# Hybrid decoder step on one core: sample tokens' projections on two column halves, their attention placed between halves of the output projection, first stage reordered

## The chip, the cores and the metric

The kernel runs on one NeuronCore of a Trainium2 chip. The core has TensorE (PE: matrix products and transposes), VectorE (DVE), ScalarE (ACT), GpSimd (POOL) and SyncE (SP, here only an issuer of transfers), each with its own instruction stream. They share SBUF (128 partitions), eight PSUM banks of 128 x 512 f32 and 16 DMA engines, and wait for each other through semaphores. All data is f32, so a product of 512 columns leaves two records of about 0.43 us. The metric is device time in microseconds of one execution; lower is better.

## The reference, cut to what is computed

One layer for two groups of tokens: a prompt of 512 tokens (one sequence) and 64 sample tokens (8 sequences of 8 tokens with stored states). Width 1024, 4 retention heads of 128.

```
mod = silu(c) @ w_mod + b_mod                       # per sequence: sh1 sc1 g1 sh2 sc2 g2
u = rmsnorm(x, n_pre1) * (1 + sc1) + sh1
z = u @ w_in;  xr, yg, q, k, v, g = split(z)
out_a = rglru(causal_conv(xr)) * gelu(yg)           # 512 channels
q, k = rotary(q) * DK**-0.5, rotary(k)
o, s_last = retention(q, k, v, s0)                  # per head, see below
out_b = groupnorm(o) * ret_gn_w * silu(g)
x = x + g1 * rmsnorm(concat(out_a, out_b) @ w_out, n_post1)
u2 = rmsnorm(x, n_pre2) * (1 + sc2) + sh2
x = x + g2 * rmsnorm(moe(u2), n_post2)              # top-2 of 4 in one of 4 groups, 16 experts
```

Retention in chunks of c tokens (128 in the prompt, 8 in a sample sequence), with decay gamma of the head:

```
inner = (q k^T * mask) v
cross = q s0 * gamma^(i+1)                          # s0: 128 x 128 state of the sequence and head
s_last = gamma^c * s0 + k^T (w_state * v)
```

For the sample tokens there are 8 sequences x 4 heads = 32 states (2 MB) to read, use and write.

## The kernel before

**Tiling.** Tokens lie in TILES = 5 tiles: four of 128 prompt tokens, and tile 4 with NS = 64 sample tokens. `x` holds them by rows, `uT` transposed, 128 channels by 576 tokens, in 8 channel steps (KT). Weights stream through `ring`, nine slots of 1 MB; SyncE issues the loads in the fixed order of `weight_pieces`, each as soon as the piece that held its slot is used up.

**The stages on TensorE** (each engine's instructions are written out in its own order; there is no scheduler):

1. First stage. Transposes of the set-up rows into bank 0, `turn_x` for each tile, `scale_part(h, i)` and `scale_sum(h)` (scale and shift of the first norm, two halves h of the channels, four parts each, with 32-row operands `cT` on four column groups of the array), `first_tiles(h)` (24 products of 288 tokens by 128 channels: channel tiles 0 to 2 of the convolution input, channel half h). Then in turn `gate_products(m)` (64x64 blocks of the RG-LRU gates), `by_channel(c, m)` (16 products of 288), `mod_step(gq, k)` (the other modulation rows, in two groups gq of 8 steps, accumulated in bank 4). VectorE runs `conv`, `rg_lru`, `gated` and `mod_rows` in a fixed order; `mod_rows(1)` empties bank 4 and frees it for `mod_step(2, 0)`.
2. Projections. For tile t and c = 0 to 3 (q, k, v, g), `project(t, c)`: 8 products with the tile's tokens stationary and 512 weight columns moving. Between them the attention of tile t-1: `turn_qk`, `scores`, `outputs`, `turn_out`. ScalarE's `take` empties the banks, VectorE's `rotate`, `mask`, `advance` and `group_norm` follow.
3. Attention of tile 4, once `turn_out(3)` is issued: `turn_qk(4)`, `scores(4)`, `sample_outputs`. The last goes head by head: one product with v, 8 of 8 columns with the states `s0` (two buffers, so GpSimd loads state h only when h-2 is stored), 2 of 512 columns for the state's increment from `vblk` (v of the 64 tokens spread over 8 blocks). VectorE's `sample_states` adds and scales, then TensorE transposes the result back, `group_norm(4)`, `turn_out(4)`.
4. Output. `out_proj(t)`: two halves c of 8 products of 512 (row names `hy`, `outbT`), then `turn_u2(t-1)`: 8 transposes, a wait for ScalarE's `take_u2T`, and 8 router products of 20 columns (row names `wrt,uT`). ScalarE's `square_m`, `square_x` and VectorE's `after_mixer(t)` make `x` and `u2` of the tile; `after_mixer(0)` also waits for all state stores (`s_ssto`).
5. Routing, then 16 experts of 128 slots each, gather of the two results per token, and the last norm.

Lines L632 and L635 are the helpers `mm` and `turn` that issue every product and transpose; L1068 is the helper of every ScalarE operation.

## Time and profile before

| | us |
|---|---|
| median of 3 runs | 695.72 (691.23 to 701.94) |
| the profiled execution | 693.1 |
| its span, first to last instruction | 691.3 |
| TensorE busy | 586.9 (85%) |
| VectorE busy | 216.2 (31%) |
| ScalarE busy | 168.6 (24%) |
| GpSimd busy | 85.2 (12%) |
| DMA, over the span | 131.45 MB, 190 GB/s |

The page divides the span into 40 slices of 17.3 us, and names the chain of work that ended last. A row of the timeline gives start, duration, engine, line, operation, output<-inputs (program's names), form and count; in brackets the idle time of the engine just before it and what ended it. `arena` is the shared work space in which most temporary tiles lie.

### The profile page before, as it was taken

The page shows a single profiled execution, that of the slowest core. Times are in us where ns is not written, and L with a number is a line of the kernel's source. Part 1 is how long each engine was busy: PE and PEld are TensorE (multiplying, and loading weights), DVE is VectorE, ACT ScalarE, POOL GpSimd, SP SyncE. Part 2 cuts the span into 40 slices and gives each one's busy share as a digit, 9 for nine tenths or more (in the row PEclk, how much of TensorE's full clock was granted, in tenths as well). Part 3 has the DMA queues.
Part 4 walks back from the last instruction along what each step waited for, and adds up shares of the span by engine and source line. Part 5 has one row for each costly group of instructions (what it writes and reads, how often), then busy time and mean ns, then how long its engine had stood idle before and what let it go on. Part 6 is the DMA issues. An engine that isn't in the chain of part 4 may idle for free.

```text
span 691.3 us, 6321 instructions
## 1 busy us (share of the span) xinstructions
PE 586.9 (85%) x2385; PEld 358.8 (52%) x2385; DVE 216.2 (31%) x495; ACT 168.6 (24%) x326; POOL 85.2 (12%) x123
## 2 busy tenths in 40 slices
PE   1897997999999999987798889339999999999700
PEld 1565654544545453465344443228777777777400
DVE  2514664120333241423314222541212121312137
ACT  3602875012222222210112211311111111112143
POOL 3104000072000000033000000220101010100060
PEclk9899999999999999955599999659999999999955
DMA  9999366794000003853200000825999999993283
GB/s 313 368 337 287 123 243 244 261 350 147 1 0 1 0 1 121 282 173 107 62 0 40 22 30 30 305 63 186 348 344 379 356 361 357 370 358 135 91 271 138
DMA packets 65155, 131.45 MB, mean 190 GB/s; under 512 B 4287, under 2 KB 37239, under 8 KB 63075
## 3 DMA queue, kind: packets, MB, share of 16 engines
q1 hardware_dynamic: 53264, 94.64, 39.0%
q0 software_dynamic: 8080, 23.15, 10.9%
q10 hardware_dynamic: 3778, 13.23, 4.9%
q8 instruction: 21, 0.34, 0.2%
q14 instruction: 12, 0.09, 0.0%
HBM read 115.32 MB, written 15.69 MB: 190 GB/s over the span
## 4 chain that ended last, share of the span: by engine, by line
PE 80%; DVE 7%; ACT 4%; DMA 4%; issue 2%; POOL 1%; DVEq 0%; POOLq 0%; ACTq 0%
PE bank L632 76%; PE bank L635 5%; ACT arena L1068 3%; DMA hy<-in_norm_pre_mix_dram 1%; DMA arena<-slots_dram,tok_slot 1%; ACT uT L1068 1%; DVE arena L1758 1%; DMA arena<-in_state_ret_dram 1%; DMA arena<-u_dram,slot_tok 1%; DMA out_dram<-arena 1%; DVE arena L1880 1%; ACT ss L1068 0%; DVE rtb L1701 0%; ACT L1068 0%; POOL arena L620 0%
## 5 line engine op out<-in xcount | busy, mean ns | idle before, releaser
L632 PE MATMUL bank<-ring,arena 128*128 128x256 f32 (+1 forms) x640 | 173.3, 427 | 2.1 <-DVE arena L1839 1.3
L1068 ACT ACTIVATE arena<-bank 128x512 f32<-128x512 f32 (+5 forms) x117 | 54.1, 493 | 364.1 <-PE bank L632 340.4
L632 PEld LDWEIGHTS bank<-ring,arena 128*128 128x128 f32 x640 | 120.3, 192 | 38.6 <-issue 25.8
L632 PE MATMUL bank<-ring,uT 128*128 128x512 f32 (+1 forms) x320 | 140.2, 593 | 0.0
L632 PEld LDWEIGHTS bank<-ring,uT 128*128 128x128 f32 (+1 forms) x320 | 56.1, 180 | 72.6 <-issue 72.3
L632 PE MATMUL bank<-uT,ring 128*128 128x288 f32 x256 | 68.6, 431 | 3.1 <-ACT uT L1068 3.1
L632 PEld LDWEIGHTS bank<-uT,ring 128*128 128x128 f32 x256 | 51.1, 202 | 18.8 <-issue 4.1
L635 PE MATMUL bank<-con,arena 128*128 128x128 f32 (+1 forms) x304 | 44.6, 287 | 14.6 <-DVE arena L1673 4.2
L635 PEld LDWEIGHTS bank<-con,arena 128*128 128x128 f32 (+1 forms) x304 | 37.4, 150 | 36.0 <-issue 22.1
L632 PE MATMUL bank<-arena 128*128 128x128 f32 (+4 forms) x216 | 46.7, 367 | 5.1 <-DMA arena<-in_state_ret_dram 3.9
L632 PEld LDWEIGHTS bank<-arena 128*128 128x128 f32 (+2 forms) x216 | 35.9, 246 | 18.6 <-issue 9.0
L632 PE MATMUL bank<-ring,hy 128*128 128x512 f32 (+1 forms) x80 | 44.1, 704 | 0.5 <-issue 0.5
L1068 ACT ACT_TABLE_LOAD x32 | 41.1, 1283 | 6.0 <-issue 5.5
L1864 DVE TENSOR_TENSOR arena<-arena,bank 128x256 f32<-128x256 f32 x16 | 6.7, 422 | 103.4 <-ACT arena L1068 103.4
L632 PE MATMUL bank<-ring,outbT 128*128 128x512 f32 (+1 forms) x80 | 36.0, 592 | 0.0
L609 POOL DMA_INDIRECT arena<-u_dram,slot_tok x16 | 16.4, 1023 | 152.1 <-DVE slot_tok L1833 147.1
L632 PEld LDWEIGHTS bank<-ring,hy 128*128 128x128 f32 (+1 forms) x80 | 16.6, 213 | 23.9 <-issue 23.9
L632 PE MATMUL bank<-ring,rowsT 128*32 128x512 f32 x192 | 23.9, 633 | 3.7 <-DVE arena L1461 3.7
L1068 ACT ACTIVATE arena<-bank,con 128x128 f32<-128x128 f32 (+1 forms) x40 | 11.4, 366 | 59.9 <-PE bank L632 53.0
L1846 DVE COPY arena<-bank 128x512 f32<-128x512 f32 x16 | 11.1, 692 | 46.7 <-PE bank L632 46.7
L632 PEld LDWEIGHTS bank<-ring,outbT 128*128 128x128 f32 (+1 forms) x80 | 14.4, 180 | 20.0 <-issue 20.0
L1652 DVE RECIPROCAL ss<-ss 128x1 f32<-128x1 f32 (+1 forms) x5 | 0.8, 161 | 65.9 <-ACT ss L1068 65.9
(182 smaller groups left out, 405.7 us busy)
## 6 DMA issues: line engine op xcount, KB each, us to landing
ring<-in_w_mod_dram SPq DMA_DIRECT2D x24, 1024.0 KB, 9.6
ring<-in_w_exp_gate_dram SPq DMA_DIRECT2D x16, 1024.0 KB, 13.0
ring<-in_w_exp_up_dram SPq DMA_DIRECT2D x16, 1024.0 KB, 11.7
ring<-in_w_exp_down_dram SPq DMA_DIRECT2D x16, 1024.0 KB, 7.8
ring<-in_w_in_dram SPq DMA_DIRECT2D x12, 1024.0 KB, 14.5
slots_dram<-arena ACTq DMA_DIRECT2D x16, 512.0 KB, 6.9
ring<-in_w_out_dram SPq DMA_DIRECT2D x4, 1024.0 KB, 6.1
x<-in_x_prompt_dram ACTq DMA_DIRECT2D x4, 512.0 KB, 10.2
```

The lines of the kernel that those rows point to most:

```text
L609: pool.indirect_dma_start(out=xg[e % 2], out_offset=None, in_=u2_dram, in_offset=bass.IndirectOffsetOnAxis(ap=slot_tok[:, e:e + 1], axis=0))\
L632: return nc.tensor.matmul(out, lhsT, rhs, start=first, stop=last)
L635: return nc.tensor.transpose(out, src, ident[0:src.shape[0], 0:src.shape[0]])
L1068: return nc.scalar.activation(out, src, func, **kw).then_inc(done, 1)
L1652: link(v.reciprocal(ss[0:n, 1, t, 0:1], ss[0:n, 1, t, 0:1]))
L1758: v.scalar_tensor_tensor(out=Y[0:n, t], in0=Y[0:n, t], scalar=ss[0:n, 3, t, 0:1], in1=tab["g2" + tag(t)][0:n], op0=ALU.mult, op1=ALU.mult) ...
L1846: v.tensor_copy(eo[e % 2][:, 512:1024], bank[5][:]).then_inc(s_eod, 1)
L1864: v.tensor_tensor(out=hg[e % 2], in0=hb[e % 2], in1=bank[e % 2][:, FE:2 * FE], op=ALU.mult).then_inc(s_hm, 1)
L1880: v.scalar_tensor_tensor(out=Y[0:n, t], in0=og[1][0:n, t], scalar=rm2[0:n, t:t + 1], in1=Y[0:n, t], op0=ALU.mult, op1=ALU.add).then_inc(s_ ...
```

## The change

- `project(4, c)`: the 64 token columns are loaded twice, into array columns 0 to 63 and 64 to 127, and each half gets 256 of the 512 weight columns: even heads on partitions 0 to 63, odd heads on 64 to 127. Everything of tile 4 up to `group_norm` is then 128 partitions by 256 columns instead of 64 by 512, and the constants follow that layout.
- Attention of tile 4: `sample_outputs` is replaced by `turn_sample_qk`, `sample_scores`, `sample_inner`, `sample_cross(p)` (p = pair of heads; four products of 512 columns on four column groups, each 32 tokens against the states of 4 sequences), `state_step(h)` and `turn_sample_out`. VectorE's `add_cross(p)` picks each token's own sequence from the cross products by a mask and adds them to the inner part; `new_state(h)` does in one operation what took two.
- These pieces stand between halves of the output projection (`out_half(t, c)`), and `turn_u2` is split from `route`. ScalarE, VectorE and GpSimd follow in orders written out to match. `after_mixer(0)` no longer waits for the state stores. Squares go to `u2` instead of a tile of their own, and the arena grows by 4 KB per partition so that `u2`, the tables and the prompt's state `S` move apart.
- First stage: the set-up transposes are split in two (`cT` first, the others after `scale_part(0, 0)`, in bank 1); `first_tiles` is dissolved into `first_tile(h, n, m)`, with the scale products of the second half between; each `by_channel` stands ahead of its `gate_products`; `mod_rows(1)` comes before `rg_lru(3)`; ScalarE takes x tiles later and runs the gelus between the sigmoids.

```diff
                 if h == 0 and i == 0:
+                    pe.wait_ge(s_cT, 1)
+                if h == 0 and i == 2:
                     pe.wait_ge(s_rowsT, 1)
                 if h == 1 and i == 0:
                     pe.wait_ge(s_scaled, 1)
...
             scale_part(0, 0)
+            turn_rows()
             turn_x(2)
...
+            for m in range(3):
+                first_tile(0, 0, m)
+            first_tile(0, 1, 0)
+            scale_part(1, 0)
+            scale_part(1, 1)
+            first_tile(0, 1, 1)
+            scale_part(1, 2)
+            scale_part(1, 3)
+            scale_sum(1)
+            first_tile(0, 1, 2)
+            for m in range(3):
                 for n in range(2):
-                    for m in range(3):
...
+            by_channel(0, 3)
             gate_products(0)
-            by_channel(0, 3)
+            by_channel(1, 0)
             gate_products(1)
-            by_channel(1, 0)
...
+                    wk = w[k // 4][:, k % 4, :]
+                    if t < TILES - 1:
+                        last = mm(bank[c][:], uT[:, k, t * P:(t + 1) * P], wk, k == 0, k == KT - 1)
+                    else:
+                        by_parity = wk.rearrange("p (a z e) -> p z a e", z=2, e=DK)
+                        for z in range(2):
+                            last = mm(bank[c][z * NS:(z + 1) * NS, 0:2 * DK], uT[:, k, SEQ:NTOK],
+                                      by_parity[:, z], k == 0, k == KT - 1)
...
+            def sample_scores():
+                pe.wait_ge(s_qkTe, TILES)
+                pe.wait_ge(s_sm, TILES - 1)
                 for h in range(NH):
-                    c = slice(h * DK, (h + 1) * DK)
-                    o = bank[7][:, h * NS:(h + 1) * NS]
-                    pe.wait_ge(s_s0[h % 2], 16 * (h // 2 + 1))
-                    mm(o, vv[0][0:NS, c], sm[0:NS, h * NS:(h + 1) * NS], True, False)
-                    for b in range(DB):
-                        q0 = h * P + b * DT
-                        last = mm(o[:, b * DT:(b + 1) * DT], s0[h % 2][:, b, :], qT[:, q0:q0 + DT],
-                                  False, b == DB - 1)
-                    last.then_inc(s_cross, 1)
-                    pe.wait_ge(s_vblk, h + 1)
-                    for n in range(2):
-                        i = 2 * h + n
-                        if i >= 2:
-                            pe.wait_ge(s_snew, i - 1)
-                        elif i == 0:
-                            pe.wait_ge(s_obTe, t)
-                        mm(bank[4 + n][:], kr[0][0:NS, c],
-                           vblk[0:NS, 4 * n:4 * n + 4, :].rearrange("p b e -> p (b e)"),
-                           True, True).then_inc(s_skv, 1)
-
-                pe.wait_ge(s_oTe, 1)
+                    z, c = h % 2, slice(h * NS, (h + 1) * NS)
+                    last = mm(bank[6][z * NS:(z + 1) * NS, h // 2 * NS:(h // 2 + 1) * NS],
+                              kT[:, c], qT[:, c], True, True)
+                last.then_inc(s_sc, 1)
...
+            def sample_inner():
+                pe.wait_ge(s_sm, TILES)
+                pe.wait_ge(s_pe, 4 * (TILES - 1) + 3)
+                pe.wait_ge(s_ob, TILES - 1)
                 for h in range(NH):
-                    last = turn(bank[6][0:NS, h * P:(h + 1) * P], sm[:, h * NS:(h + 1) * NS])
+                    z, p = slice(h % 2 * NS, (h % 2 + 1) * NS), h // 2
+                    last = mm(bank[7][z, p * DK:(p + 1) * DK], sm[z, p * NS:(p + 1) * NS],
+                              vv[0][z, p * DK:(p + 1) * DK], True, True)
                 last.then_inc(s_o, 1)
...
+            def sample_cross(p):
+
+                if p == 0:
+                    pe.wait_ge(s_sm, TILES)
+                else:
+                    pe.wait_ge(s_lg, 1)
+                for z in range(2):
+                    pe.wait_ge(s_s0[z], 16 * (p + 1))
+                    for half_b in range(2):
+                        q0 = (2 * p + z) * NS + half_b * 32
+                        g = z * NS + half_b * 32
+                        last = mm(bank[6][g:g + 32, :], qT[:, q0:q0 + 32],
+                                  s0[z][:, 4 * half_b:4 * half_b + 4, :]
+                                  .rearrange("p b e -> p (b e)"), True, True)
+                last.then_inc(s_cross, 1)
...
+            def state_step(h):
+                z = slice(h % 2 * NS, (h % 2 + 1) * NS)
+                pe.wait_ge(s_vblk, h // 2 + 1)
...
+                for n in range(2):
+                    mm(bank[4 + n][:], kr[0][z, h // 2 * DK:(h // 2 + 1) * DK],
+                       vblk[z, 4 * n:4 * n + 4, :].rearrange("p b e -> p (b e)"),
+                       True, True).then_inc(s_skv, 1)
...
+                    if t and c == 2:
+                        outputs(t - 1)
+                    if t and t < TILES - 1 and c == 3:
+                        turn_out(t - 1)
+            turn_sample_qk()
...
+                if 1 <= t:
+                    pe.wait_ge(s_obTe, t + 1)
...
+            out_half(0, 0)
+            turn_out(TILES - 2)
+            sample_scores()
+            out_half(0, 1)
+            sample_inner()
+            sample_cross(0)
+            out_half(1, 0)
+            state_step(0)
+            out_half(1, 1)
+            state_step(1)
+            out_half(2, 0)
+            turn_u2(0)
+            out_half(2, 1)
+            route(0)
+            turn_u2(1)
+            sample_cross(1)
+            out_half(3, 0)
+            route(1)
+            turn_sample_out()
+            state_step(2)
+            out_half(3, 1)
+            turn_u2(2)
+            out_half(4, 0)
+            route(2)
+            state_step(3)
+            out_half(4, 1)
+            turn_u2(3)
+            route(3)
+            turn_u2(4)
+            route(4)
...
+            take_u2T(0)
+            square_m(2)
+            take_u2T(1)
+            deviation(TILES - 1)
+            square_x(2)
+            store_u2(2)
+            take_sample_obT()
+            square_m(3)
+            take_u2T(2)
+            square_x(3)
+            store_u2(3)
+            square_m(4)
+            take_u2T(3)
+            square_x(4)
+            store_u2(4)
+            take_u2T(4)
...
             conv(3)
             rg_lru(2)
             gated(0)
+            mod_rows(1)
             rg_lru(3)
-            mod_rows(1)
             for m in range(1, MT):
                 gated(m)
...
+            def add_cross(p):
...
+                dve.wait_ge(s_cross, p + 1)
+                dve.wait_ge(s_o, TILES)
+                acc, inner = qr[:, p * DK:(p + 1) * DK], bank[7][:, p * DK:(p + 1) * DK]
+                link(v.tensor_copy(acc, inner))
+                for j in range(4):
+                    last = v.scalar_tensor_tensor(
+                        out=acc, in0=bank[6][:, j * DK:(j + 1) * DK],
+                        scalar=con[:, C_XM + j:C_XM + j + 1], in1=acc,
+                        op0=ALU.mult, op1=ALU.add)
+                    link(last) if j < 3 else last.then_inc(s_acc, 1)
...
+            def new_state(h):
...
+                dve.wait_ge(s_cross, h // 2 + 1)
+                for n in range(2):
+                    part = s0[h % 2][:, 4 * n:4 * n + 4, :].rearrange("p b e -> p (b e)")
+                    dve.wait_ge(s_skv, 2 * h + n + 1)
+                    v.scalar_tensor_tensor(out=part, in0=part, scalar=GAMMA_STEP[h],
+                                           in1=bank[4 + n][:], op0=ALU.mult, op1=ALU.add)\
+                        .then_inc(s_snew, 1)
...
-                    dve.wait_ge(s_ssto, 16 * NH)
...
+            mask(TILES - 1)
+            add_cross(0)
+            after_mixer(0)
+            new_state(0)
+            new_state(1)
+            after_mixer(1)
+            take_logits(0)
+            add_cross(1)
+            group_norm(TILES - 1)
+            after_mixer(2)
+            take_logits(1)
+            new_state(2)
+            after_mixer(3)
+            take_logits(2)
+            new_state(3)
+            after_mixer(4)
+            take_logits(3)
+            take_logits(4)
```

TensorE in the first stage. `bank<-uT,ring` are the products of the tiles (16 to a `by_channel`), `ring,rowsT` the scale or modulation products, `con,arena` with 32 columns the sums, `arena,wgate` the gates; the number at the end counts instructions. Before:

```order
L632 MATMUL bank<-con,arena 128x32 x8
L632 MATMUL bank<-uT,ring 128x288 x24
L632 MATMUL bank<-ring,rowsT 32x512 x16
L632 MATMUL bank<-con,arena 128x32 x8
L632 MATMUL bank<-uT,ring 128x288 x24
L632 MATMUL bank<-arena,wgate 64x512 x2
```

And with the change:

```order
L642 MATMUL bank<-con,arena 128x32 x8
L642 MATMUL bank<-uT,ring 128x288 x16
L642 MATMUL bank<-ring,rowsT 32x512 x8
L642 MATMUL bank<-uT,ring 128x288 x4
L642 MATMUL bank<-ring,rowsT 32x512 x8
L642 MATMUL bank<-con,arena 128x32 x8
L642 MATMUL bank<-uT,ring 128x288 x44
L642 MATMUL bank<-arena,wgate 64x512 x2
```

The second sums are now followed by 4 products of the first half, and `by_channel(0, 3)` (the last 16 of the 44) stands before the first gates.

TensorE from the end of the projections. `ring,uT` is `project(4, 3)`, `con,arena` are transposes, `ring,hy` and `ring,outbT` the two halves of depth of an output projection. Before:

```order
L632 MATMUL bank<-ring,uT 64x512 x8
L635 MATMUL bank<-con,arena 128x128 x4
L635 MATMUL bank<-con,arena 128x64 x8
L632 MATMUL bank<-arena 64x64 x4
L632 MATMUL bank<-arena 128x64
L632 MATMUL bank<-arena 128x8 x8
L632 MATMUL bank<-arena 128x512 x2
```

And with the change:

```order
L642 MATMUL bank<-ring,uT 64x256 x16
L645 MATMUL bank<-con,arena 128x128 x4
L642 MATMUL bank<-ring,hy 128x512 x4
L642 MATMUL bank<-ring,outbT 128x512 x4
L645 MATMUL bank<-con,arena 128x128 x4
L642 MATMUL bank<-arena 64x64 x4
L642 MATMUL bank<-ring,hy 128x512 x4
L642 MATMUL bank<-ring,outbT 128x512 x4
L642 MATMUL bank<-arena 64x128 x4
L642 MATMUL bank<-arena 32x512 x4
L642 MATMUL bank<-ring,hy 128x512 x4
L642 MATMUL bank<-ring,outbT 128x512 x4
```

The first half of the output projection has moved ahead of the last prompt tile's `turn_out` and of the sample scores; inner and cross products of the samples follow the second half.

VectorE at the same place, with the change (before, the rows of L1763, L1765 and L1777 did not exist, and `after_mixer(0)` followed the samples' `group_norm`): `mask(4)`, `add_cross(0)`, `after_mixer(0)`, then the new states 0 and 1.

```order
L1698 TENSOR_TENSOR arena<-bank,con 128x128
L1763 COPY arena<-bank 128x128
L1765 SCALAR_TENSOR_TENSOR arena<-bank,con,arena 128x128 x4
L1797 RECIPROCAL ss<-ss 128x1
L1802 SCALAR_TENSOR_TENSOR arena<-bank,ss,arena 128x512 x2
L1807 TENSOR_TENSOR x<-x,arena 128x1024
L1810 RECIPROCAL ss<-ss 128x1
L1814 SCALAR_TENSOR_TENSOR arena<-x,ss,arena 128x1024
L1817 TENSOR_TENSOR arena<-arena 128x1024
L1777 SCALAR_TENSOR_TENSOR arena<-arena,bank 128x512 x4
```

The last row holds both states together, ahead of tile 1's `after_mixer`.

## Rows read from the trace of the kernel before

**Rows 1.** The page: two lines of the slices, and the chain by engine

```profile
PE   1897997999999999987798889339999999999700
...
PEclk9899999999999999955599999659999999999955
...
PE 80%; DVE 7%; ACT 4%; DMA 4%; issue 2%; POOL 1%; DVEq 0%; POOLq 0%; ACTq 0%
```

**Rows 2.** Windows: length, busy of PE, PEld, DVE, ACT, POOL; clock, DMA share, GB/s

```profile
31.00:69.00 38.00, 33.97 (x144) 23.92 (x144) 10.98 (x39) 8.85 (x21) 9.26 (x16) 0.87 0.96 315
69.00:137.00 68.00, 64.13 (x355) 38.02 (x356) 32.11 (x70) 38.62 (x56) 2.05 (x4) 0.97 0.57 214
137.00:261.00 124.00, 124.00 (x385) 62.19 (x382) 36.60 (x104) 28.01 (x59) 17.57 (x35) 1.00 0.23 74
...
294.00:339.00 45.00, 34.77 (x117) 23.44 (x116) 17.21 (x36) 3.94 (x8) 14.35 (x11) 0.53 0.43 130
339.00:432.00 93.00, 86.33 (x239) 40.05 (x240) 22.15 (x31) 17.05 (x46) 0.00 (x0) 0.91 0.06 23
...
465.00:649.00 184.00, 183.19 (x849) 138.82 (x848) 37.32 (x72) 28.98 (x63) 13.64 (x14) 0.99 0.87 303
```

**Rows 3.** Timeline of TensorE in the first stage: start, us, form, [idle before]

```profile
31.56 14.93 PE L632 MATMUL bank<-uT,ring 128*128 128x288 f32 x48 [1.56 <-ACT uT L1068]
...
53.52 13.57 PE L632 MATMUL bank<-uT,ring 128*128 128x288 f32 x48 [1.56 <-ACT uT L1068]
69.16 2.17 PE L632 MATMUL bank<-arena,wgate 64*64 64x512 f32 x16 [2.07 <-ACT arena L1068]
71.25 8.03 PE L632 MATMUL bank<-uT,ring 128*128 128x288 f32 x32
...
92.83 2.17 PE L632 MATMUL bank<-arena,wgate 64*64 64x512 f32 x16
...
120.29 4.99 PE L632 MATMUL bank<-ring,rowsT 128*32 128x512 f32 x32 [3.71 <-DVE arena L1461]
...
133.16 3.64 PE L632 MATMUL bank<-ring,rowsT 128*32 128x512 f32 x32
```

**Rows 4.** Timeline of VectorE in the first stage: `gated(0)`, ends of `mod_rows(1)`

```profile
104.66 0.75 DVE L1519 TENSOR_TENSOR hy<-hy,arena 128x576 f32<-128x576 f32 x1
...
118.28 0.41 DVE L1457 TENSOR_SCALAR arena<-arena 64x512 f32<-64x512 f32 x1
...
119.45 0.69 DVE L1461 TENSOR_TENSOR arena<-arena 128x512 f32<-128x512 f32 x1
```

**Rows 5.** Timeline of TensorE: `project(4, 0)`, `turn_out(3)`, first output group

```profile
260.98 7.08 PE L632 MATMUL bank<-ring,uT 128*64 128x512 f32 x16
...
294.01 0.66 PE L635 MATMUL bank<-con,arena 128*128 128x128 f32 x4
...
339.36 6.44 PE L632 MATMUL bank<-ring,hy 128*128 128x512 f32 x8 [0.52 <-issue]
```

**Rows 6.** Groups of weight loads by form: busy us, mean ns, idle before

```profile
L632 PEld LDWEIGHTS bank<-ring,uT 128*64 128x64 f32 x64 | 8.4, 137 | 16.9 <-issue 16.7
```

**Rows 7.** Timeline of TensorE in the output stage, around `turn_u2(0)` and the end

```profile
369.66 1.04 PE L635 MATMUL bank<-con,arena 128*128 128x128 f32 x8
372.80 1.96 PE L632 MATMUL bank<-wrt,uT 128*128 128x20 f32 x16 [2.11 <-ACT uT L1068]
374.61 5.38 PE L632 MATMUL bank<-ring,hy 128*128 128x512 f32 x8
...
427.67 3.60 PE L632 MATMUL bank<-ring,outbT 128*64 128x512 f32 x8
```

**Rows 8.** Timeline of VectorE: the last operation of `after_mixer(1)`

```profile
377.74 1.22 DVE L1673 TENSOR_TENSOR arena<-arena 128x1024 f32<-128x1024 f32 x1
```

**Rows 9.** DMA issues of the page: count, KB each, median us to landing

```profile
arena<-in_state_ret_dram POOLq DMA_DIRECT2D x4, 512.0 KB, 5.2
out_dram<-arena POOLq DMA_DIRECT2D x4, 512.0 KB, 3.9
```

433 lines of the change are left out of this document (228 added, 205 removed).

## The prediction

> **What bounds the kernel now.** I read the page's slices first, then the chain, the windows by stage, TensorE's timeline at the seams, and last ScalarE, VectorE and GpSimd beside it. The chain that ended last is TensorE for 80% of the span [rows 1], and the slices show it busy nearly throughout, with two holes: slices 18 to 20 and 26 to 27 (counted from 1), where the granted clock is also half [rows 1]. The second is the routing behind the output stage, which the change leaves alone. The windows put names to it [rows 2]. From 294 to 339 us (the sample tokens' attention, nothing else) TensorE is busy 34.77 of 45 us at a clock of 0.53; from 339 to 432 (output projection) 86.33 of 93 at 0.91; from 31 to 137 (first stage) about 98 of 106 at 0.87 and 0.97. The middle, 137 to 261, has no gap, and the experts, 465 to 649, are 183.19 of 184 busy at 0.99. The change touches the three stages that have slack and leaves alone the two that have none; the DMA share is 0.06 in the output stage and 0.43 in the sample stage, so bytes aren't the bound there.
>
> **First stage.** The new order takes away three waits of TensorE [rows 3]. Before `first_tiles(1)` it stood 1.56 us for the scale of the second half, and then ran 13.57 us for 24 products that take 12.0 at the full clock (16 take 8.03), so 1.57 was clock. Now four products of the first half (2 us) stand between the sum and that point, and cover those 1.56. `gate_products(0)` waited 2.07 for the first convolution; `by_channel(0, 3)`, 8 us, now covers it. `mod_step(2, 0)` waited 3.71 for `mod_rows(1)`, which stood behind `rg_lru(3)` on VectorE, and then ran 4.99 for what takes 3.64 when the clock is full: 1.35 more. Is it really free now? From the start of `gate_products(2)` at 92.83 [rows 3] through `rg_lru(2)` to the end of `gated(0)` at 105.41 went 12.6 us, and `mod_rows(1)` took 118.28 to 120.14, 1.9 us [rows 4]: 14.4 together. TensorE has 2.17+3.64+8.03+2.17 = 16.0 us of work in the same stretch: hidden, by 1.6 us only. Sum: 1.56+1.57+2.07+3.71+1.35 = 10.3. The split of the set-up transposes I cost at nothing: tile 0's can start earlier, but the 9 small ones, formerly in an idle stretch, now stand between products, and tile 2's norm waits on VectorE behind `take_rows`, so the start of `first_tiles(0)` at 31.56 [rows 3] should move by tenths only. The clock fall at 31 us (14.93 us for the same 24 products [rows 3]) I leave in; if it went, 2.9 us more.
>
> **Projections of tile 4.** Before: 4 of 7.0 us, since 64 rows cost as much as 128 (8 products of 512 columns, two records of 0.43 each) [rows 5]. Now each is 16 products of 256 columns, in pairs on the two column halves. The trace has no 64-column pairs of full depth. Nearest above: alone, one after the other, the same 7.0. Nearest below: the 128*32 form, four beside each other, does 32 records of 512 columns in 3.64 us, 0.114 a record instead of 0.43 [rows 3]; and `gate_products` (pairs of 64x64) does 4 products of 512 and 4 of 64 columns in 2.17, where one after the other would be 3.9. Both run wholly side by side, so I take half: 8 steps x 2 passes x 0.215 = 3.5 us. Saved: 4 x 3.5 = 14.0; bounds 0 and 14.
>
> A weight load of the 64-column form takes 137 ns [rows 6]. In the four-group form four loads go with each 0.43 us of stream and cost nothing in the 3.64; here it is two per 0.215. If they could not be taken beside each other or beside the stream, a step would be 0.43+4x0.137 = 0.98 and a projection 7.8 us, longer than now: 4 x 4.3 = 17.3 us over my sum. The Trainium skill, "TensorE: Matmul & The Clock Gate", Part 3, The mechanism, says that a load overlaps running products only when its row group differs, and both halves share their rows. By that rule this edit loses; the 3.64 us of the four-group form speak against it.
>
> **Sample attention.** Everything from `turn_out(3)` at 294.01 to the first output projection at 339.36 goes from its place: 45.35 us [rows 5]. Back on TensorE's path come: 4 transposes (0.55), `turn_out(3)` (0.66), scores and inner products (0.5 each), two `sample_cross` of four 32-column groups (0.91 each, a quarter of the 3.64), four `state_step` of two 512-column products (8 x 0.86 = 6.9), the output's transposes (0.3): 11.2. One wait is new: `out_half(0, 0)` needs ScalarE's silu of the last projection. That is queued behind `deviation(3)` and a table load. Before, a projection of 7 us covered this and nothing showed; now one of 3.5 does. Bounds 0 and 3.5, I take 1.0, since most of the VectorE work ahead of it is unchanged. So 45.35-12.2 = 33.2 saved.
>
> **Output stage.** The gaps: TensorE stood 2.11 us for `take_u2T` before three of the router products [rows 7], 6.3 us, and after each the first group of 8 records took 5.38 instead of 3.60, 5.3 us; the very first took 6.44, 2.8 us. Now another half projection or a sample step is placed between each hand-over and its use. Saved 14.4.
>
> **Does the new order hide it?** I walked the new TensorE list from `project(4, 0)` = 0: first output half at 20.4, second (after transposes and scores) 28.6 to 35.4, then one piece of 6.9 us after another with the sample steps between, last half at 101.9 to 108.8; before, the same stretch was 260.98 to 431.3, 170.3. The tail behind it is unchanged. The hand-overs: from the end of a projection to `u2` ready takes 9.3 us (369.66 to 378.96) [rows 7, 8]. For tile 1 VectorE is now behind `new_state(1)`, so it starts at 55.8 rather than 54.4 and ends at 63; `turn_u2(1)` comes at 71. ScalarE's `take_u2T(0)` is queued behind `store_u2(1)`, so behind that same 63: done 64; `route(0)` needs it at 69, the tightest, 5 us. The states: a store takes 3.9 us to land and a load 5.2 [rows 9]; state 3 is there at 65, `sample_cross(1)` comes at 72. If one of these covers is gone, its lateness comes 1:1 on the path.
>
> **Sum.** 10.3+14.0+33.2+14.4 = 71.9. About 20 more hand-overs between short pieces, 0.1 us each by the seams of [rows 5]: +2. Span 691.3-71.9+2 = 621.4; the profiled execution took 1.8 us more than its span, 623.2; the median of before stands 2.6 over its profiled one: about 625.
>
> **Rivals.** Main case, 612 to 634: 0.69. (a) The halves run one after the other: nothing of the 14.0; 639. Against it the 3.64 and 2.17 us rows: 0.05. (b) The loads are exposed: 17.3 over, 642; 0.05. (c) The interleaved block waits on its helpers: VectorE has three kinds of work in one strict order (after_mixer, add_cross, new_state) where it had one, and ScalarE's copies wait behind stores; if two of the hand-overs above are late by 5 to 10 us, 632 to 650. For it: slacks of 5 to 8 us are worked out; against: VectorE is busy only 22 of 93 us there [rows 2]; 0.14. (d) The first stage keeps its total, as `mod_rows(1)` misses by its 1.6 us and the clock falls again: 635; 0.05. (e) The slow side: the clock stays at its lower level (1.2 GHz) throughout the interleaved block, as it did from 294 to 339 although TensorE was busy 77% of it with many short pieces. Then its 88 us of work from first to last half would take 88 us more: 713. With 57 us of that work at half clock the gain falls to 2%, with 71 us to nothing; the case begins there. Against: output groups right behind a gap are back at 3.60 us after one group [rows 7]; 0.02.
>
> The change is told from no change at about 2%, so faster means under 682: only (e) is not. Faster 0.97, same 0.01, slower 0.02. The range 612 to 641 takes the main case, (a), (d) and the lower half of (c).
>
> **What would show it.** In the profile after: `project(4, c)` at 3.5 us each (7.0: (a); 7.8: (b)); no wait over 0.5 us before a `mod_step`, and the first unbroken tile 0 projection near 127 us instead of 137; from `project(4, 0)` to the last output half 109 us instead of 170; the clock at 1.0 in it and the 5.38 us groups gone; the experts' 184 us and the tail unchanged. I am wrong if TensorE idles in that block by more than 5 us in sum, or if the experts' stage grows, for instance because weights land later relative to their use.

## The result, and the profile after

The changed kernel takes 625.31 us (median of 4 runs, 624.39 to 625.39), the kernel before 697.5 (691.23 to 701.94, 4 runs): ratio 0.8996, 95% interval 0.896 to 0.9032. The profiled execution took 624.39 us, its span is 622.6 where 691.3 was, 68.7 less. The forecast was 625 and a span of 621.4. Another four runs of the same kernel, on the chip of the later experiments, gave 625.91 and a span of 623.1.

The page of the changed kernel: busy time, two of the slices (now of 15.6 us), the chain by engine.

```profile
PE 542.3 (87%) x2391; PEld 336.0 (54%) x2391; DVE 213.5 (34%) x493; ACT 168.5 (27%) x322; POOL 81.1 (13%) x121
...
PE   1899999999999999999999951799999999999500
...
PEclk9889999999999999999999875699999999999855
...
PE 85%; DVE 6%; DMA 3%; ACT 2%; issue 2%; POOL 0%; DVEq 0%; ACTq 0%; POOLq 0%
```

Of the two holes of [rows 1] one is left, the routing. The windows by stage, columns as in [rows 2]: first stage (two rows), projections of the prompt tiles, the interleaved block from `project(4, 0)` to the last output half, the experts.

```profile
31.00:69.00 38.00, 36.77 (x169) 26.52 (x170) 14.42 (x46) 9.28 (x21) 9.88 (x18) 0.96 0.94 317
69.00:126.00 57.00, 57.00 (x333) 32.98 (x332) 29.77 (x64) 39.92 (x57) 2.05 (x4) 1.00 0.68 257
126.00:250.00 124.00, 123.97 (x382) 61.96 (x382) 36.20 (x104) 28.22 (x60) 17.55 (x35) 1.00 0.23 73
250.00:362.00 112.00, 111.50 (x462) 55.02 (x459) 46.73 (x95) 26.27 (x62) 12.22 (x11) 0.98 0.38 134
395.00:581.00 186.00, 184.65 (x850) 139.90 (x850) 37.87 (x73) 29.73 (x63) 14.05 (x14) 0.99 0.86 300
```

From 69 to 362 us TensorE now stands for about half a microsecond in all. The first stage, timeline of TensorE:

```profile
32.23 9.51 PE L642 MATMUL bank<-uT,ring 128*128 128x288 f32 x32 [1.56 <-ACT uT L1158]
...
49.32 10.92 PE L642 MATMUL bank<-uT,ring 128*128 128x288 f32 x44
...
110.23 3.64 PE L642 MATMUL bank<-ring,rowsT 128*32 128x512 f32 x32
...
125.78 2.74 PE L642 MATMUL bank<-ring,uT 128*128 128x512 f32 x6
```

The last row is `project(0, 0)`, 11.4 us earlier than the 137.19 us that follow from [rows 3] (133.16 plus 3.64, and 0.4 for the turn of the tails). The first row still has the wait of 1.56 us and a clock loss; the two other waits and the one ahead of `mod_step(2, 0)` (110.23) are gone. The block, the same view (the timeline of TensorE):

```profile
249.78 3.67 PE L642 MATMUL bank<-ring,uT 128*64 128x256 f32 x32
...
270.34 3.70 PE L642 MATMUL bank<-ring,hy 128*128 128x512 f32 x8 [0.50 <-ACT arena L1158]
...
293.93 1.98 PE L642 MATMUL bank<-arena 64*128 64x512 f32 x4
295.84 3.70 PE L642 MATMUL bank<-ring,hy 128*128 128x512 f32 x8
299.38 3.60 PE L642 MATMUL bank<-ring,outbT 128*128 128x512 f32 x8
...
319.53 1.86 PE L642 MATMUL bank<-wrt,uT 128*128 128x20 f32 x16
...
349.12 1.96 PE L642 MATMUL bank<-wrt,uT 128*128 128x20 f32 x16
351.01 2.12 PE L642 MATMUL bank<-arena 64*128 64x512 f32 x4
353.06 5.16 PE L642 MATMUL bank<-ring,hy 128*64 128x512 f32 x8
...
361.58 1.09 PE L645 MATMUL bank<-con,arena 128*128 128x128 f32 x8
```

`project(4, 0)` takes 3.67 us where [rows 5] has 7.08. One wait is left in the block, 0.50 us for ScalarE ahead of the first output half. At 351 to 358 us something new shows: the state products and the first output group of tile 4's second half are slow (2.12 for 1.98, 5.16 for 3.65) with no idle time ahead of them. From 249.78 to 361.58, the first transpose behind the last output half, are 111.8 us; before, from 260.98 to 431.20, 170.2.

So: first stage 11.4 less, block 58.4 less, the stretch behind it 0.9 more (261.0 us, before 260.1), the projections of the prompt tiles 0.2 more: 68.7 in sum. The stretch behind grows in one place: behind the idle time of the routing the first 32 records of the experts take 9.78 us (before 8.66). In the profiles of all the kernels below this group takes between 8.65 and 10.15 us, though no edit touches it, so a difference of 1 to 1.5 us between two single profiles can be chance of this kind.

### The profile page after: what moved, and what is told of

The parts are those of the page before. It is cut to its first block, busy times and chain, and to the rows that moved or that the text cites. A ratio compares the mean times of both kernels' runs of the same rounds, so it can differ in the third digit from the quotient of the medians.

```text
span 622.6 us, 6336 instructions
## 1 busy us (share of the span) xinstructions
PE 542.3 (87%) x2391; PEld 336.0 (54%) x2391; DVE 213.5 (34%) x493; ACT 168.5 (27%) x322; POOL 81.1 (13%) x121
## 3 DMA queue, kind: packets, MB, share of 16 engines
q0 software_dynamic: 8080, 23.16, 11.7%
## 4 chain that ended last, share of the span: by engine, by line
PE 85%; DVE 6%; DMA 3%; ACT 2%; issue 2%; POOL 0%; DVEq 0%; ACTq 0%; POOLq 0%
PE bank L642 80%; PE bank L645 6%; ACT arena L1158 1%; DMA x<-in_x_prompt_dram 1%; DMA arena<-slots_dram,tok_slot 1%; DVE arena L1915 1%; DMA arena<-u_dram,slot_tok 1%; DVE arena L2037 1%; DVE rtb L1858 1%; POOL arena L630 0%; DMA slots_dram<-arena 0%; DVE x L1919 0%; ACT L1158 0%; ACT ss L1158 0%; DVE arena L1516 0%
## 5 line engine op out<-in xcount | busy, mean ns | idle before, releaser
L642 PE MATMUL bank<-ring,uT 128*128 128x512 f32 (+1 forms) x384 | 126.8, 522 | 0.0
L642 PE MATMUL bank<-uT,ring 128*128 128x288 f32 x256 | 65.4, 415 | 1.6 <-ACT uT L1158 1.6
L642 PEld LDWEIGHTS bank<-uT,ring 128*128 128x128 f32 x256 | 49.0, 194 | 18.3 <-issue 5.0
L645 PEld LDWEIGHTS bank<-con,arena 128*128 128x128 f32 (+1 forms) x294 | 37.2, 152 | 30.3 <-issue 14.4
L642 PE MATMUL bank<-ring,hy 128*128 128x512 f32 (+1 forms) x80 | 38.3, 623 | 0.5 <-ACT arena L1158 0.5
L642 PE MATMUL bank<-arena 128*128 128x128 f32 (+4 forms) x168 | 26.1, 339 | 0.0
L642 PEld LDWEIGHTS bank<-ring,hy 128*128 128x128 f32 (+1 forms) x80 | 13.9, 184 | 21.9 <-issue 21.1
L642 PEld LDWEIGHTS bank<-ring,outbT 128*128 128x128 f32 (+1 forms) x80 | 14.4, 179 | 20.0 <-issue 20.0
L1158 ACT ACTIVATE arena<-bank,con 128x128 f32<-128x128 f32 x36 | 10.4, 368 | 53.1 <-PE bank L642 46.2
L642 PEld LDWEIGHTS bank<-arena 128*128 128x128 f32 (+4 forms) x168 | 18.2, 178 | 8.6 <-issue 8.5
L1683 DVE TENSOR_TENSOR arena<-arena,con 128x512 f32<-128x512 f32 (+1 forms) x10 | 6.3, 635 | 36.6 <-ACT arena L1158 32.8
## 6 DMA issues: line engine op xcount, KB each, us to landing
ring<-in_w_exp_up_dram SPq DMA_DIRECT2D x16, 1024.0 KB, 11.4
ring<-in_w_in_dram SPq DMA_DIRECT2D x12, 1024.0 KB, 14.7
```

The costliest lines, as they stand in the source:

```text
L642: return nc.tensor.matmul(out, lhsT, rhs, start=first, stop=last)
L645: return nc.tensor.transpose(out, src, ident[0:src.shape[0], 0:src.shape[0]])
L1158: return nc.scalar.activation(out, src, func, **kw).then_inc(done, 1)
L1683: v.tensor_tensor(out=each(dst), in0=each(src), in1=cs, op=ALU.mult)
```

## The experiments

Differences are given between the profiled spans where a single piece is read off (changed kernel: 622.6 and 623.1), and between medians where whole kernels are compared. The first stage undone, its one line undone, the serial halves and the attention in one piece were executed twice, the other kernels four times.

**The first stage undone.** The changed kernel with the old first stage, all of it:

```diff
-            by_channel(0, 3)
             gate_products(0)
+            by_channel(0, 3)
...
-            mod_rows(1)
             rg_lru(3)
+            mod_rows(1)
```

> The changed kernel with the first stage as it was before (order of TensorE, ScalarE and VectorE, one set-up transpose group). Theory: the first stage is worth 11.4 us by itself (the first projection of tile 0 started at 137.19 us before and starts at 125.78 in the changed kernel), so about 636.7 us, with the projections starting at 137 and the stretch from project(4, 0) to the last output half at 112 us unchanged. Rival: the later stages lean on the earlier start (weights on the way), and the loss is under 8 or over 15 us. If the sum of terms was only right by luck, this run shows another number than 10 to 12.

Measured 638.12 us (636.86 to 639.38), span 635.1. TensorE:

```profile
68.56 2.02 PE L640 MATMUL bank<-arena,wgate 64*64 64x512 f32 x11 [2.07 <-ACT arena L1146]
...
119.70 6.20 PE L640 MATMUL bank<-ring,rowsT 128*32 128x512 f32 x32 [3.71 <-DVE arena L1569]
...
137.81 4.46 PE L640 MATMUL bank<-ring,uT 128*128 128x512 f32 x10
```

The waits of [rows 3] are back with the same lengths, the products behind the last of them take 6.20 us instead of 3.64, and `project(0, 0)` starts 12.0 us later. The theory holds: 12.5 us by the spans. The block takes 113.5 us instead of 111.8, since the fall of the clock in it costs 3.3 us here and 1.65 there.

**The first stage alone**, in the kernel before: the same edits the other way round.

> The kernel before with the new first stage alone: the products of the small gate projections a stage earlier, gates(t) set between them, the new order of VectorE's entries there. Everything from the projections of the sample tokens on is as before. My theory: the change's parts add up without touching each other. The first stage gave 12.0 us in undo_first and 11.4 us between the profiles of before and after, and it gives the same here: ratio to before 0.983 (an estimate: 11.7 of 693), span about 680. Rival: part of the gain is only real because the stages after it were made shorter (in the kernel before, the sample tokens' block waits for VectorE and the first output groups ran at half clock, so a start 11 us earlier could turn into waits there): then 3 to 6 us only, ratio 0.991 to 0.996, and a longer idle time shows ahead of the output groups.

Measured 682.08 us (681.67 to 689.86); ratio to before 0.9873, interval 0.9792 to 0.9954; span 680.3, 11.0 less than before. `project(0, 0)` starts at 125.55 us, the last output half ends 12.5 us earlier. The forecast was a ratio of 0.983; the interval touches the 0.991 of the rival, and by time alone the gain isn't clear of 2%. What excludes the rival is the trace: ahead of the output groups TensorE waits 4.19 and 0.52 us, as before (4.18 and 0.52), so the earlier start isn't turned into waits there. The parts add: about 11 to 12 us here and 12 in the full kernel.

**One line of it undone.**

```diff
             gated(0)
-            mod_rows(1)
             rg_lru(3)
+            mod_rows(1)
             for m in range(1, MT):
```

> The changed kernel with mod_rows(1) back behind rg_lru(3) on VectorE, nothing else. Theory A, from the rows of before: it undoes a wait of 3.7 us and a clock loss of 1.35, so +5 us, 630.4. Theory B: in the new order by_channel(1, 2) stands ahead of the gate products, so from the start of gate_products(3) (108.14) VectorE needs the 13.8 us that it took before (106.45 to 120.29) and TensorE has 2.2 us of other work: a wait of 11.6 us, with some 1.5 to 3 us at the lower clock behind it: +13 to +15, about 639. B says that this one line carries more than the whole first stage gains.

Measured 638.6 us (638.41 to 638.79), span 637.0. TensorE, and VectorE's last operation of `mod_rows(1)`:

```profile
122.20 6.34 PE L642 MATMUL bank<-ring,rowsT 128*32 128x512 f32 x32 [11.67 <-DVE arena L1591]
```
```profile
121.36 0.69 DVE L1591 TENSOR_TENSOR arena<-arena 128x512 f32<-128x512 f32 x1
```

Theory B holds: the wait is 11.67 us and the fall of the clock behind it 2.7 more: 14.7 us at `project(0, 0)`, which starts 3.3 us later than in the kernel before. This is more than the whole first stage gains, since gates and convolution products have moved ahead of `mod_step(2, 0)` and no longer stand behind it as cover. The placing of `mod_rows(1)` isn't one part of five that could be left out: without it the new order loses more than its other parts gain.

**The halves one after the other.** Same products, same shapes, but all eight steps of the even heads, then all of the odd:

```diff
-                        for z in range(2):
+                    for z in range(2):
+                        for k in range(KT):
                             last = mm(bank[c][z * NS:(z + 1) * NS, 0:2 * DK], uT[:, k, SEQ:NTOK],
```

> The changed kernel with the loop over the two column halves outside the loop over the 8 steps in project(4, c), so that neighbouring products lie on the same half; same products, same weight loads, same layout. Theory: the saving comes from neighbours on different halves streaming at the same time. Then each of the four takes 7.0 to 7.1 us instead of 3.60, and the 0.5 us wait ahead of the first output half goes: +13.3 to 13.8, about 638.8 us. Rival: the saving comes from the halved width alone (256 instead of 512 columns moving) and neighbours don't matter: 625.

Measured 634.47 us (632.68 to 636.25), span 630.9. TensorE:

```profile
249.89 6.32 PE L642 MATMUL bank<-ring,uT 128*64 128x256 f32 x32
...
280.40 3.70 PE L642 MATMUL bank<-ring,hy 128*128 128x512 f32 x8
...
361.06 1.98 PE L642 MATMUL bank<-arena 64*128 64x512 f32 x4
362.97 3.65 PE L642 MATMUL bank<-ring,hy 128*64 128x512 f32 x8
```

6.32 us each instead of 3.67: 10.6 more in four. Against it, 0.5 of the wait ahead of the first output half is gone, and so is the late fall of the clock (1.65): 8.4, and the span is 8.3 longer. So neighbours on different column halves do run at the same time, and it is the alternating that gives it. The size that I gave (638.8 us, 7.0 a projection) was off: 32 records in 6.32 us are 0.197 each, under the 0.215 that half of a 0.43 us record would be.

**The samples' attention in one piece**, ahead of the first output half:

```diff
-            out_half(0, 0)
             turn_out(TILES - 2)
             sample_scores()
-            out_half(0, 1)
             sample_inner()
             sample_cross(0)
-            out_half(1, 0)
             state_step(0)
-            out_half(1, 1)
             state_step(1)
+            sample_cross(1)
+            turn_sample_out()
+            state_step(2)
+            state_step(3)
+            out_half(0, 0)
...
```

> The changed kernel with all sample pieces (scores, inner, cross and state products, their VectorE and ScalarE work) in one block ahead of the output projection instead of between its halves; same instructions, waits adapted. Theory (place): the pieces are short on TensorE (12 us) but chained through VectorE, and the second pair of states needs two stores and two loads (3.9 and 5.2 us each, GpSimd in series); out of cover the block takes some 33 us and the output stage starts at half clock: +20 to +27, 645 to 652 us. Rival (form): the new forms alone gave the saving, the place is worth under 8 us: below 633. The granted clock in the block tells a third thing: if it falls, many short products or the gaps let it fall.

Measured 656.09 us (652.42 to 659.76), span 650.6. TensorE, and the window of the attention:

```profile
289.74 1.92 PE L642 MATMUL bank<-arena 128*32 128x512 f32 x4 [6.45 <-DMA arena<-in_state_ret_dram]
295.52 1.92 PE L642 MATMUL bank<-arena 128*32 128x512 f32 x4 [3.86 <-DMA arena<-in_state_ret_dram]
301.81 0.69 PE L645 MATMUL bank<-con,arena 128*128 128x128 f32 x2 [4.37 <-DVE arena L1734]
302.43 3.77 PE L642 MATMUL bank<-arena 64*128 64x512 f32 x4
...
310.75 5.64 PE L642 MATMUL bank<-ring,hy 128*128 128x512 f32 x8
```
```profile
268.00:311.00 43.00, 22.04 (x65) 6.94 (x62) 15.50 (x39) 4.71 (x8) 10.00 (x9) 0.65 0.49 170
```

In this place the new form of the attention takes 42.2 us (268.51 to 310.75), hardly less than the 45.35 of the old one. TensorE is busy 22.04 of 43 us at a clock of 0.65, with eight waits of 20.9 us together, of which 10.3 us are loads of states 2 and 3 behind the stores of 0 and 1. The 656.09 lie above the 645 to 652 that I expected, as the 42.2 lie above the 33. The new form without the new place gives 3 us; the place gives another 28 by the spans, with what it saves in the output stage. It doesn't follow that the form is worth 3 us in the new place: the old form between the output halves was never run. An estimate from the rows: before, TensorE was busy 34.77 us of this stretch at a mean clock of 0.53 [rows 2], some 18 us at the full clock, and the new pieces take 12 us in the block, so there the form may be worth about 6 us.

**The routing unsplit**: both output halves of a tile, then `route` behind its `turn_u2` without an output half between. ScalarE's `take_u2T(0)` moves ahead of `square_x(1)` to match; the rest is as changed.

```diff
-            out_half(2, 0)
             turn_u2(0)
-            out_half(2, 1)
             route(0)
+            out_half(2, 0)
+            out_half(2, 1)
...
```

> The changed kernel with one thing of its block undone: all output halves of tile t run one after the other and then route(t-1), as in the kernel before, so that the 128x20 router products and the turns of u2 no longer have an output half between them and what they wait for. My theory from the rows of before (2.11 us of wait ahead of a tile's router products, and the output groups behind it 1.8 us longer at half clock), three times: 3 x 2.1 + 3 x 1.8 = 11.7, so 637 us. Rival: the placing of the routes is worth little, because the sample tokens' attention that now lies between the halves is what fills the gap and keeps the clock: 2 us or less, 625 to 627.5. Both are told apart by the idle time before turn_u2 and route and by the granted clock of the output halves behind them.

Measured 638.94 us (637.45 to 640.79, 4 runs), span 635.6. TensorE around the second of them:

```profile
329.96 2.96 PE L642 MATMUL bank<-wrt,uT 128*128 128x20 f32 x16 [2.16 <-DVE arena L1767]
332.76 6.01 PE L642 MATMUL bank<-ring,hy 128*128 128x512 f32 x8
```

Waits of 0.87, 0.74, 2.16 and 2.11 us, 5.9 in sum; output groups of 5.27, 6.01 and 5.40 instead of 3.60 to 3.70, and router products of 2.08, 2.96 and 3.49 instead of 1.9: 8.6 at the lower clock. Less the 1.65 of the fall that the changed kernel has, that is 12.8; the span is 13.0 longer. The rival, 2 us or less, is out. Here, too, a wait costs more than its length: behind 5.9 us of idle time TensorE lost another 8.6 to the clock. That isn't a rate: the 11.67 us of the run with `mod_rows(1)` late cost 2.7 more, the three places here 1.9, 3.4 and 3.3.

**The fall of the clock without a wait.** First the changed kernel once more:

> The changed kernel itself once more, on the chip on which the next three run, so that they are compared with it on one chip: 625 us, between 622 and 629, with the fall of TensorE's granted clock at about 353 us without an idle gap ahead of it. If that fall is a matter of chance, it is missing or elsewhere here.

625.91 us (624.69 to 627.96). The fall is there again at the same place (353.15 us, 5.34 for the first group). Then with one step moved on TensorE, and on VectorE `new_state(3)` ahead of `take_logits(2)`:

```diff
             out_half(4, 0)
-            route(2)
             state_step(3)
             out_half(4, 1)
+            route(2)
             turn_u2(3)
...
+            new_state(3)
             take_logits(2)
-            new_state(3)
```

> The changed kernel with one step moved: the router products of tile 2 (route(2), 16 products of 20 columns, 1.9 us) go from ahead of state_step(3) to behind the last output half, and VectorE's read of them behind new_state(3). It asks two things. First, the fall of TensorE's granted clock at 351 to 358 us, which has no idle gap ahead of it and cost 1.7 us in both profiles of the changed kernel. In every profile so far in which it came without a gap, a group of router products and then a 64-row state_step of 2 us stood ahead of it, and with state_steps of 1.1 us it was gone. Theory A: it is that pair that brings it; with route(2) away the stretch keeps 2.4 GHz and the last output half of tile 4 takes 3.65 us in its first group. Theory B: it follows something else (VectorE, DMA, time of the day of the chip): it comes again within 10 us of the same place, and the first group of the output half or its neighbour takes 5 us or more. Second, route(2) behind the last output half lies in the time in which TensorE waits for squares and normalisation of tile 3 and tile 4, so its 1.9 us leave the path. Sum by A: 1.7 + 1.9 = 3.6, 622.0 us; by B: 623.7; if VectorE's read of route(2) delays the squares of tile 4, 0.5 to 1 us less.

```profile
348.95 1.98 PE L642 MATMUL bank<-arena 64*128 64x512 f32 x4
350.86 3.65 PE L642 MATMUL bank<-ring,hy 128*64 128x512 f32 x8
...
357.87 1.96 PE L642 MATMUL bank<-wrt,uT 128*128 128x20 f32 x16
```

The fall is gone, the last output half ends 3.7 us earlier, and the span is 619.0, 3.6 and 4.1 under the two profiles of the changed kernel. The executions took 620.52, 620.86, 627.5 and 627.6 us (median 624.18, nearer to the 623.7 of theory B than to the 622.0 of A), so the timing alone doesn't separate it from the changed kernel. Only the one of 620.86 us was profiled, and the trace says nothing of the other three. Does it show the cause? Only in part. Router products ahead of a 2 us `state_step` were there in every profile with such a fall (the changed kernel twice, the one with the first stage undone at 363 us, the one with `mod_rows(1)` late at 365 us, and the next but one below at 333 us, with two transposes between). But the same pair, with the two transposes, stood at 332 us in the changed kernel, and at 359 us in the one with serial halves, without a fall. With the state steps of 1.1 us of the next run, no fall came without a wait. By these runs the pair goes with such a fall but doesn't suffice for it; what decides is open. Nor is a fall that stays away always saved: with serial halves and in the next run it comes one place later, in the router products of tile 3 behind their wait of 1.94 us (3.01 and 3.38 us instead of 1.96), where it costs nothing, since TensorE waits for VectorE right behind them anyway.

**State products of two heads beside each other.** Head 2p lies on rows 0 to 63, head 2p+1 on rows 64 to 127:

```diff
-                for n in range(2):
-                    mm(bank[4 + n][:], kr[0][z, h // 2 * DK:(h // 2 + 1) * DK],
-                       vblk[z, 4 * n:4 * n + 4, :].rearrange("p b e -> p (b e)"),
+                for z in range(2):
+                    q = slice(z * NS, (z + 1) * NS)
+                    mm(bank[4 + z][:], kr[0][q, p * DK:(p + 1) * DK],
+                       vblk[q, 4 * n:4 * n + 4, :].rearrange("p b e -> p (b e)"),
```

> The changed kernel with the state products of two heads beside each other: a head's keys and values are on 64 of the 128 rows, head 2p on rows 0 to 63 and head 2p+1 on rows 64 to 127, and the two products of one state_step go to two banks from the two row halves instead of from one row half twice. Eight products of 512 columns in four steps, 1.98 us a step in the changed kernel's profile. My theory: what sits beside each other on different rows runs at the same time, as the column halves of the projections did: a step takes about 1.0 us, four steps save 3.6 to 4, 621.5 us. Rival: the row halves are already overlapped, or are not run together: no change, 625. Price of a mishap: new_state comes later for each first head of a pair, and its state is stored after the pair: if the end of a store gated anything on TensorE, there would be a wait ahead of the last output half.

Measured 618.79 us (617.49 to 619.99, 4 runs), span 616.7; the changed kernel beside it 625.91.

```profile
293.51 1.13 PE L643 MATMUL bank<-arena 64*128 64x512 f32 x4
...
348.02 1.13 PE L643 MATMUL bank<-arena 64*128 64x512 f32 x4
349.08 3.65 PE L643 MATMUL bank<-ring,hy 128*64 128x512 f32 x8
```

1.13 instead of 1.98 us: 3.4 in four steps. Row halves run beside each other as column halves do. The gain is larger than the forecast (621.5): of the 6.4 us between the spans 3.4 are the state steps and 1.7 the fall of the clock, which is gone as well; 0.7 lie ahead of the block and 0.6 behind it, where the edit changes nothing.

**The samples' output projection on two column halves**, into one bank:

```diff
+                for k in range(KT):
+                    src = hy[:, k] if k < MT else outbT[:, k - MT]
+                    for c in range(2):
+                        w = weights(pe, ("out", c, k // 4)).rearrange("p (k n) -> p k n", n=512)
+                        last = mm(bank[0][c * NS:(c + 1) * NS, :], src[:, SEQ:NTOK],
+                                  w[:, k % 4, :], k == 0, k == KT - 1)
```

> The changed kernel with what it does to the sample tokens' projections done to their output projection too: the two column halves of the 64-token tile go side by side on the two column halves of the array, into one bank, 64 products of 512 columns in pairs. Two groups of 7.1 us each in the profile of the changed kernel. My theory: 32 pairs at the rate of the paired projections (3.67 us for 16 pairs) are 7.3 us, so 14.2 - 7.3 = 6.9 saved on TensorE, and of VectorE's and ScalarE's work behind it (squares and residual of 64 tokens in two halves) up to 2 us more can lie in the open or be hidden: 616 to 619, I say 617.5. Rival A: that half was hidden behind new_state on VectorE, whose end sets when the next stage may start: then what is saved turns into a wait ahead of route(4) and the experts, 623 to 625. Rival B: the other half of a bank's rows costs the readers (ScalarE and VectorE read their half from the partitions 64 to 127): no gain and up to 2 us more.

Measured 617.06 us (615.01 to 623.43, 4 runs), span 617.2.

```profile
332.73 2.67 PE L647 MATMUL bank<-arena 64*128 64x512 f32 x4
335.33 6.35 PE L647 MATMUL bank<-ring,hy 128*128 128x512 f32 x8
...
345.92 3.65 PE L647 MATMUL bank<-ring,hy 128*64 128x512 f32 x16
349.40 3.60 PE L647 MATMUL bank<-ring,outbT 128*64 128x512 f32 x16
```

Both halves together take 7.0 us where one took 7.0: the full 7.0 are saved on TensorE. At 333 us the clock fell (3.3 us), earlier than in the changed kernel although TensorE's program is the same up to there. Rival A came true for a small part: TensorE now waits 0.87 us for `new_state(3)` and then runs the router products of tile 3 in 3.60 us instead of 1.96, but tile 4's turn still starts 6.3 us earlier. Rival B is out.

**Both**, and **both with `route(2)` behind `state_step(3)`**:

```diff
-            route(2)
             state_step(3)
+            route(2)
...
-            take_logits(2)
             new_state(3)
+            take_logits(2)
```

> state_pairs and out4_pair together. If both theories hold and neither hides the other, the savings add: 3.8 + 7 = 10.8, 614.5 us. If VectorE's chain behind the last state product sets the start of the experts, the sum is short by what waits there, up to 6 us: then 618 to 621.

> both with route(2) behind state_step(3) instead of ahead of it, and VectorE's new_state(3) ahead of its read of route(2). In both, TensorE waited 1.54 us for new_state(3) behind state_step(3) and then ran the turns and the router products of tile 3 at 1.2 GHz (3.60 us instead of 1.96). Theory: route(2) covers that wait, and new_state(3) comes 2 us earlier, so VectorE starts on tile 4 up to 1.0 us earlier: 0.5 to 1.5 us faster than both, 611.0 us. Rival: VectorE's work on tile 4 starts when ScalarE's squares are there and not when new_state(3) is done, or it waits for the read of route(2) instead: no change, 611.9.

611.93 us (611.23 to 617.91) and 611.74 us (611.46 to 612.79; ratio to before 0.8791, interval 0.874 to 0.8843), spans 610.1 and 609.9: both beat the changed kernel by 14 us. The two edits add: by the spans beside that of the changed kernel on the same chip, 6.4 and 5.9 us alone and 13.0 together. The forecast of 614.5 for both was 2.6 us too careful; it didn't count the fall of the clock, 1.7 us in the changed kernel, which is gone in this profile. The last step brought nothing (611.0 was forecast), as the rival said. TensorE with the swapped order, and VectorE:

```profile
351.98 2.09 PE L648 MATMUL bank<-wrt,uT 128*128 128x20 f32 x16 [1.09 <-ACT uT L1176]
358.12 1.12 PE L651 MATMUL bank<-con,arena 64*128 64x64 f32 x8 [4.05 <-DVE arena L1836]
```
```profile
350.85 0.15 DVE L1816 RECIPROCAL ss<-ss 64x1 f32<-64x1 f32 x1 [0.66 <-ACT ss L1176]
```

The wait for `new_state(3)` and the slow router products went, but tile 4's turn waits for VectorE's chain on tile 4, and that began at 350.85 instead of 351.22 us, now held by ScalarE's squares. TensorE is no longer the bound in this place.

## Why the prediction was right, step by step

- **First stage, 10.3 forecast, 11.4 measured.** The three waits (1.56, 2.07, 3.71) and two clock losses (1.57, 1.35) went as forecast. The loss at 31 us I had left in, at 2.9 or nothing; it is 1.5 now (9.51 us for 16 products of 8.03), 1.4 less. That is not the new order's doing: with the old first stage put back, the same 24 products took 13.57 us at this place, 1.6 over 12.0, so the 14.93 of [rows 3] is not tied to the old order. Against that the start is 0.67 later. Sum 11.0, the rest is seams. The margin of `mod_rows(1)`, forecast 1.6 us, is 1.35: its last operation ends at 108.88, `mod_step(2, 0)` starts at 110.23. What it is worth I had not seen: rival (d) priced a miss at 10 us as if the whole stage stood alone, and the one-line run shows 14.7.
- **Projections of tile 4, 3.5 forecast, 3.67 measured** (3.60 from start to start). Rival (b), exposed loads, would have made it 7.8; the row excludes it. The Trainium skill, "TensorE: Matmul & The Clock Gate", Part 3, The mechanism, says that a load overlaps running products only when its row group differs; the same section also names a load into the background weight buffer as one that is pulled ahead. The two halves share their rows, so the trace doesn't agree with the first of these; into which buffer a load goes no run shows. The rows of before could have settled it: from 137 to 261 us TensorE is busy 124.00 of 124.00 us beside 62.19 us of loads [rows 2], nearly all for products over all 128 rows. Rival (a) falls as well; its bound of 7.0 was too high, serial halves take 6.32.
- **Sample attention, 33.2.** `state_step` takes 1.98 and not 1.72 (1.91 from start to start), +0.7 in four; the wait for the silu is 0.50 and not 1.0. The mechanism stands: in one piece the same work costs 42.2 us. The 33.2 mix the form and the place; how they share it is only estimated (run in one piece).
- **Output stage, 14.4.** The gaps are gone and so are the 5.38 us groups, all but one. The unsplit run gives 12.8 to 13.0 back for a part expected at 11.7 (3 x 2.1 and 3 x 1.8): there the router products ran at the lower clock too (up to 3.49 us), which in the kernel before they didn't (1.96).
- **The walk through the hand-overs.** VectorE starts tile 1's `after_mixer` 55.75 us after `project(4, 0)`, forecast 55.8, and ends at 65.0, forecast 63. `take_u2T(0)` is done at 66.5 and `route(0)` comes at 69.75: 3.2 us of slack where I had 5. The difference is one VectorE operation (below). No hand-over was late; rival (c) is out, with less room than I thought.
- **Clock in the block** (e): 0.98 in the window, so (e) is out. Not foreseen: the fall at 353 us.
- **The experts.** The prediction called a longer experts' stage a sign of being wrong. It is 1.1 us longer, all of it in its first 32 records (9.78 us, before 8.66), and nothing in it waits longer for weights. With the first stage undone this group takes 8.65 us, so the growth doesn't belong to the new block.
- **Sum.** Block 108.8 plus 2 for hand-overs forecast, 111.8 measured: the fall of the clock 1.65 over, output halves of 6.87 to 7.07 us instead of 6.9 +1.0, state steps +0.7, projections +0.4, inner and cross products +0.2, silu -0.5: 3.4 by the rows and 3.0 by the ends over the 108.8, of which the hand-overs had 2. First stage 1.1 better, the stretch behind 0.9 worse: the errors are about 1 us each and partly cancel, and the span is 1.2 over the forecast (622.6 for 621.4). The hit on the median (625.0 for 625.3) is luck on top of that: the sum as written comes to 623.2 + 2.6 = 625.8 and was rounded down, and the 2.6 that the median of before stood over its profiled execution are 0.9 in the changed kernel.

## What to carry to other kernels

Where a stage with many short pieces waits for its helpers, put the pieces between long products of the next stage before making them cheaper: here the new form in one piece gave 3 us and its place between the output halves another 28. Price a wait of TensorE with the clock that it can cost, here from nothing to 3.4 us for a wait of 1.6 to 12 us, and not in proportion to its length, and ask of each reordered wait which products stood behind it and now stand ahead. Matrices that use half of the array's columns or rows are worth pairing wherever two independent ones are neighbours: projections, output projection and state products all gave nearly the full half.

## What was not expected of the hardware

**A VectorE operation of 1.28 us took 3.40** while GpSimd spread v over the blocks. VectorE and GpSimd of the changed kernel:

```profile
310.13 3.40 DVE L1814 SCALAR_TENSOR_TENSOR arena<-x,ss,arena 128x1024 f32<-128x1024 f32 x1
```
```profile
310.53 1.91 POOL L582 TENSOR_TENSOR arena<-arena,con 128x1024 f32<-128x1024 f32 x1
```

The same operation took 1.28 to 1.29 us for the other tiles. In all eight profiles in which GpSimd's starts 0.4 us into it, it took 3.40 us. In the run with paired states GpSimd's came at 311.46 us, beside nothing of VectorE's, and VectorE's took 1.28 us, as in the three other profiles in which they don't meet. It is 2.1 us longer, about GpSimd's 1.91. The Trainium skill, "SBUF — State Buffer", SBUF: two separate sides, says that a VectorE instruction with two SBUF inputs and a GpSimd instruction that reads SBUF lock each other out for a whole instruction, whichever starts first going on. The trace agrees with the lock-out; that the one that had started 0.4 us earlier was the one held up does not fit, in any of the eight, but GpSimd's spans are rough.

**The clock fell with TensorE never idle**, behind router products of 20 columns and 64-row products, for 1.65 and 1.7 us in the changed kernel, 1.65 in a third kernel and 3.3 in two others. It was gone in the one profile with the router products moved; why the same pair stays harmless elsewhere is open.

**Products for 64 of the 128 columns, one after the other,** took 0.197 us a record of 256 columns where 0.215 is half a record of 512. Why they are quicker no run here shows.
